# Two-block decoder on one Trainium2 core: a new step sequence for the recurrence pairs, crossed 64-row halves in the triangular inverse, and two-pass suffix sums in the stick-breaking heads

## The reference, cut to what matters

```python
# stick-breaking: 8 heads of 128, twice
u = jnp.where(mask, jax.nn.softplus(z), 0.0)
a = jnp.where(mask, jnp.exp(z - _rev_cumsum(u)), 0.0)   # suffix sums over the keys

# recurrence, per head and token
sa = jnp.einsum('bhvk,bhk->bhv', S, -kk_t)
S = S * w_t[:, :, None, :] + sa[..., None] * (kk_t * a_t)[:, :, None, :] + v_t[..., None] * k_t[:, :, None, :]
o = jnp.einsum('bhvk,bhk->bhv', S, r_t)
```

## Time and profile before

| | us |
|---|---|
| median of 3 runs | 3991.29 (3989.72 to 3993.7) |
| profiled execution, its own time | 3987.37 |
| span of its trace | 3985.6 |
| TensorE busy | 3749.2 |
| VectorE / ScalarE / GpSimd busy | 1779.6 / 1319.2 / 299.8 |
| mean granted TensorE clock | 0.974 of full |

### The profile page before, as it was taken

One profiled execution on the slowest core, in us unless ns is written; L12 is line 12 of the kernel. 1 busy time (PEld: TensorE's weight loads), 2 busy tenths in 40 slices (PEclk: granted clock), 3 DMA queues, 4 the chain that ended last, 5 costly groups with the idle time before them and its releaser, 6 DMA issues.

```text
span 3985.6 us, 52849 instructions
## 1 busy us (share of the span) xinstructions
PE 3749.2 (94%) x22827; PEld 3045.0 (76%) x22827; DVE 1779.6 (45%) x2457; ACT 1319.2 (33%) x2020; POOL 299.8 (8%) x328
## 2 busy tenths in 40 slices
PE   7999999988899999999999999998989998599999
PEld 6777888766688877888887778886867677478887
DVE  4323434444543445443443244344645656445443
ACT  4343322332332232332334332224332323333222
POOL 1011101000110111110100111011000000000001
PEclk9999999999999999999999999998999999799999
DMA  6212333311232332233231132322121221333332
GB/s 205 69 48 69 95 95 95 96 54 45 76 95 91 94 90 87 94 99 97 93 93 43 53 95 88 107 92 82 55 72 50 82 59 54 102 116 89 102 96 68
DMA packets 333229, 337.39 MB, mean 85 GB/s; under 512 B 11858, under 2 KB 323780, under 8 KB 332485
## 3 DMA queue, kind: packets, MB, share of 16 engines
q1 hardware_dynamic: 332578, 333.89, 27.4%
q10 hardware_dynamic: 418, 0.12, 0.0%
HBM read 319.29 MB, written 14.68 MB: 84 GB/s over the span
## 4 chain that ended last, share of the span: by engine, by line
PE 85%; DVE 7%; ACT 5%; issue 2%; DMA 1%; ACTq 0%; POOL 0%; SPq 0%; POOLq 0%; DVEq 0%
PE P L99 84%; DVE lo L117 2%; ACT hi L113 1%; PE P L102 1%; ACT sA L114 1%; DVE rw_S L117 0%; DVE x L117 0%; DVE LG L117 0%; ACT rw_S L114 0%; DVE rw_kk L117 0%; DVE rw_k L117 0%; DVE ds L125 0%; DVE mp L122 0%; ACT L111 0%; DMA scr<-held_dram 0%
## 5 line engine op out<-in xcount | busy, mean ns | idle before, releaser
L117 DVE TENSOR_TENSOR lo<-raw,hi 128x1024 fp32r<-128x1024 f32 (+2 forms) x617 | 739.4, 1199 | 1200.7 <-ACT hi L113 1200.0
L99 PE MATMUL P<-aH,lo 128*128 128x512 f32 x2840 | 1140.5, 402 | 15.0 <-DVE aL L125 7.1
L99 PE MATMUL P<-aL,hi 128*128 128x512 f32 x2840 | 1113.4, 392 | 0.0
L99 PE MATMUL P<-aH,hi 128*128 128x512 f32 x2840 | 1113.3, 392 | 0.0
L113 ACT ACTIVATE hi<-raw 128x1024 fp32r<-128x1024 f32 (+2 forms) x617 | 610.7, 991 | 1055.0 <-PE P L99 1048.3
L99 PEld LDWEIGHTS P<-aH,lo 128*128 128x128 f32 x2840 | 538.5, 190 | 144.8 <-issue 21.0
L99 PEld LDWEIGHTS P<-aL,hi 128*128 128x128 f32 x2840 | 538.5, 190 | 113.1 <-issue 6.4
L99 PEld LDWEIGHTS P<-aH,hi 128*128 128x128 f32 x2840 | 537.4, 189 | 114.0
L99 PE MATMUL P<-bH,lo 128*128 128x512 f32 x1088 | 426.5, 392 | 14.9 <-DVE bL L117 14.9
L99 PE MATMUL P<-bL,hi 128*128 128x512 f32 x1088 | 425.3, 391 | 0.0
L99 PE MATMUL P<-bH,hi 128*128 128x512 f32 x1088 | 425.1, 391 | 0.0
(11 more groups left out here) (276 smaller groups left out, 3906.5 us busy)
## 6 DMA issues: line engine op xcount, KB each, us to landing
raw<-in_w_ffn_in_dram SPq DMA_DIRECT2D x176, 512.0 KB, 3.5
raw<-in_w_in_dram SPq DMA_DIRECT2D x163, 512.0 KB, 3.8
raw<-in_w_ffn_out_dram SPq DMA_DIRECT2D x96, 384.0 KB, 3.0
raw<-in_w_ffn_dram SPq DMA_DIRECT2D x36, 512.0 KB, 3.7
raw<-in_w_o_dram SPq DMA_DIRECT2D x26, 512.0 KB, 3.4
raw<-in_w_ffn_dram SPq DMA_DIRECT2D x32, 384.0 KB, 3.1
raw<-in_w_mem_kv_dram SPq DMA_DIRECT2D x16, 512.0 KB, 3.9
raw<-in_w_ffn_out_dram SPq DMA_DIRECT2D x16, 512.0 KB, 3.4
```

Source lines behind the costliest of these rows:

```text
L99: return self.e.matmul(out, l, r, start=start, stop=stop, skip_group_check=skip) if self.e else Nothing()
L117: return self.e.tensor_tensor(out, a, b, op) if self.e else Nothing()
```

## The change

1. **Sequence of a pair.** The numbers in `pair_steps` change, `rw_square` moves behind projection v and leaves its first half (VectorE product, ScalarE square) as a new step `rw_unit`; `rw_turn_v` moves behind projection r. Banks are dealt out anew.
2. **Crossed halves.** `across` takes the place of `blocks` in `rw_level_a`, `rw_level_b`, `rw_init` and the last part of `rw_solve` (11 of the 16 sets that `blocks` issued in a pair): head h=1 is kept with its two chunks exchanged, so that each of the four combinations of input half and output half occurs, and the results go to two banks, by input half. `rw_level_c` keeps equal halves. A set of 8 products (`Z0`) and a ScalarE copy turn the start value of one head; on VectorE `rw_first` has one operation of 512 columns for two of 256, and two smaller ones.
3. **Stick-breaking sums.** The masked softplus is split into `sH` (ScalarE copy to float32r) and `sL` (VectorE subtraction, written in place over `sA`), in a new step `stick_split`, by banks. The ten float32 products become twenty float32r ones with the constants copied once to `cR`. The first diagonals are zeroed bank by bank.

```diff
-        out += [Step("stick_scores", l, h, u, pe=2.2, lat=8.5, needs=[("qkv", l, h // 2)]),
-                Step("stick_sums", l, h, u, pe=4.4, lat=4.0),
+        out += [Step("stick_scores", l, h, u, pe=2.2, lat=7.0, needs=[("qkv", l, h // 2)]),
+                Step("stick_split", l, h, u, lat=3.5), Step("stick_sums", l, h, u, pe=2.5, lat=4.0),
...
     out = [Step("rw_begin", p, u)]
-    out += proj("k", 1, 0, 1.0)
-    out += [Step("rw_lora", p, u, pe=3.4, lat=4.0), Step("rw_square", p, u, pe=0.9, lat=0.5)]
-    out += proj("v", 2, 1, 3.0)
-    out += [Step("rw_key", p, u), Step("rw_turn_v", p, u, pe=0.45, lat=0.5)]
-    out += proj("r", 0, 2, 4.0)
-    out += [Step("rw_decay", p, u, pe=0.9, lat=3.0)]
-    out += [Step("rw_turn", p, u, n, pe=0.45, lat=(3.0, 0.8, 0.6)[n]) for n in range(3)]
-    out += [Step("rw_gram", p, u, n, pe=1.8, lat=1.2) for n in range(2)]
+    out += proj("k", 1, 1, 0.0)
+    out += [Step("rw_lora", p, u, pe=2.6), Step("rw_unit", p, u)]
+    out += proj("v", 2, 2, 0.0)
+    out += [Step("rw_square", p, u, pe=0.9), Step("rw_key", p, u)]
+    out += proj("r", 0, 1, 0.0)
+    out += [Step("rw_turn_v", p, u, pe=0.45, lat=3.0), Step("rw_decay", p, u, pe=0.9, lat=2.4)]
+    out += [Step("rw_turn", p, u, n, pe=(0.6, 0.45, 0.45)[n], lat=(1.0, 1.0, 0.6)[n]) for n in range(3)]
+    out += [Step("rw_gram", p, u, n, pe=0.9, lat=(1.1, 2.3)[n]) for n in range(2)]
...
     for n in range(1, 6):
-        out += [Step("rw_level_a", p, u, n, pe=0.9, lat=1.8)]
+        out += [Step("rw_level_a", p, u, n, pe=0.5 if n > 1 else 1.2, lat=0.9)]
         if n < 5:
-            out += [Step("rw_level_b", p, u, n, pe=0.9, lat=0.0)]
+            out += [Step("rw_level_b", p, u, n, pe=0.5)]
...
     for ck in range(8):
-        out += [Step("rw_step_a", p, u, ck, pe=0.4, lat=1.0), Step("rw_step_b", p, u, ck, pe=0.7, lat=0.7 if ck < 7 else 1.6)]
+        out += [Step("rw_step_a", p, u, ck, pe=0.25, lat=0.55), Step("rw_step_b", p, u, ck, pe=0.6, lat=0.3 if ck < 7 else 3.0)]
...
+            for n, A in enumerate((m["sH"][u], m["sL"][u])):
+                e.wait_ge(*(S.act_attn, S.dve_attn)[n].at(("stick", l, h, b)))
+                t = e.mm(P[:, B + b, o:o + w], tri, A[:, DIAG[j]:DIAG[j] + w], False, True, True)
...
+    def across(u, l, r, back):
+
+        for q in range(4):
+            for h in range(2):
                 for x in range(2):
-                    rows, cs = slice(64 * x, 64 * x + 64), slice(256 * h + 64 * q, 256 * h + 64 * q + 64)
-                    t = e.mm(P[rows, 3 * u + b, cs], l(h, q)[rows], r(h, q)[rows], True, True, True)
-        return t
+                    s, t = (h ^ x, x) if back else (x, h ^ x)
+                    i = e.mm(P[64 * t:64 * t + 64, 3 * u + s, 64 * q:64 * q + 64], l(h, q, s), r(h, q, s), True, True, True)
+        return i
...
+    def stick_split(l, h, u):
+        A, H = m["sA"][u], m["sH"][u]
+        for b, o, w in FLAT:
+            e.wait_ge(*S.diagonal.at((l, h, b)))
+            e.act(H[:, o:o + w], A[:, o:o + w], ACT.Copy).then_inc(*S.act_attn.up(("stick", l, h, b)))
...
+    def stick_split(l, h, u):
+        A, H, L = m["sA"][u], m["sH"][u], m["sL"][u]
+        for b, o, w in FLAT:
+            e.wait_ge(*S.act_attn.at(("stick", l, h, b)))
+            e.tt(L[:, o:o + w], A[:, o:o + w], H[:, o:o + w].bitcast(F32), ALU.subtract).then_inc(*S.dve_attn.up(("stick", l, h, b)))
```

More of the change, by code:

```diff
@@ L821, in rw_turn @@
     def rw_turn(p, u, n):
-        A, j = m["rw"][u], (0, 2, 1)[n]
+        A = m["rw"][u]
         e.wait_ge(*S.rw_dve[u].at((p, ("KR0", "nb", "kd")[n])))
-        take(3 * u + j)
-        turn(3 * u + j, (A["KR"][:, 0, :], A["aa"], A["S2"])[n], (p, "turn", n), u)
-        rw_free(u, j, S.rw_act[u], (p, "nat", n))
+        if n:
+            j = (2, 0)[n - 1]
+            take(3 * u + j)
+            turn(3 * u + j, (A["aa"], A["S2"])[n - 1], (p, "turn", n), u)
+            rw_free(u, j, S.rw_act[u], (p, "nat", n))
+            return
+        take(3 * u, 3 * u + 1)
+        for q in range(4):
+            for h in range(2):
+                for x in range(2):
+                    t = e.mm(P[half(h, x), 3 * u + h, 64 * q:64 * q + 64],
+                             A["KR"][half(h, 0), 0, 128 * q + 64 * x:128 * q + 64 * x + 64], ident[half(h, 0), half(h, 0)],
+                             True, True, True)
+        t.then_inc(*S.rw_product[u].up((p, "turn", 0)))
+        for j in range(2):
+            rw_free(u, j, S.rw_act[u], (p, "nat", 0))
     def rw_gram(p, u, n):
-        A, js = m["rw"][u], ((0, 2), (1, 0))[n]
+        A, js = m["rw"][u], ((2, 1), (0, 2))[n]
         src = (A["aa"], A["S2"])[n]
@@ L870, in rw_level_a @@
         e.wait_ge(*S.rw_dve[u].at((p, "T", n - 1)))
-        take(3 * u)
-        blocks(u, 0, cut((A["cs"], A["S1"])[n % 2]), cut(A["k"])).then_inc(*S.rw_product[u].up((p, "U", n)))
+        take(3 * u, 3 * u + 1)
+        across(u, plain((A["cs"], A["S1"])[n % 2]), paired(A["k"]), False).then_inc(*S.rw_product[u].up((p, "U", n)))
         rw_free(u, 0, S.rw_act[u], (p, "U", n))
+        rw_free(u, 1, S.rw_act[u], (p, "U", n))
+        if n == 1:
+            take(3 * u + 2)
+            for q in range(4):
+                for x in range(2):
+                    t = e.mm(P[half(1, x), 3 * u + 2, 64 * q:64 * q + 64], paired(A["k"])(1, q, x), ident[half(0, x), half(0, x)],
+                             True, True, True)
+            t.then_inc(*S.rw_product[u].up((p, "Z0")))
+            rw_free(u, 2, S.rw_act[u], (p, "Z0"))
     def rw_level_b(p, u, n):
@@ L878, in rw_level_b @@
         e.wait_ge(*S.rw_dve[u].at((p, "Z", n - 1)))
-        take(3 * u + 1)
-        blocks(u, 1, cut(A["kk"]), cut(A["S0"])).then_inc(*S.rw_product[u].up((p, "dT", n)))
+        e.wait_ge(*S.rw_act[u].at((p, "Z0")))
+        take(3 * u, 3 * u + 1)
+        across(u, plain(A["kk"]), paired(A["S0"]), True).then_inc(*S.rw_product[u].up((p, "dT", n)))
+        rw_free(u, 0, S.rw_dve[u], (p, "T", n))
         rw_free(u, 1, S.rw_dve[u], (p, "T", n))
@@ L1290, in rw_lora, with rw_unit @@
         e.act(A["g"], bank(3 * u), ACT.Copy).then_inc(*mine.up((p, "g")))
[L1292 removed]
+    def rw_unit(p, u):
         A = m["rw"][u]
@@ L1318, in rw_turn, with two @@
         e.wait_ge(*S.rw_product[u].at((p, "turn", n)))
-        e.act(m["rw"][u]["nat"][:, n, :], bank(3 * u + (0, 2, 1)[n]), ACT.Copy).then_inc(*S.rw_act[u].up((p, "nat", n)))
+        out = m["rw"][u]["nat"][:, n, :]
+        if n:
+            e.act(out, bank(3 * u + (2, 0)[n - 1]), ACT.Copy).then_inc(*S.rw_act[u].up((p, "nat", n)))
+        else:
+            e.act(two(out), P[:, 3 * u:3 * u + 2, 0:256], ACT.Copy).then_inc(*S.rw_act[u].up((p, "nat", n)))
+    def two(x):
+        return x.rearrange("p (b f) -> p b f", b=2)
     def rw_level_a(p, u, n):
@@ L1335, in rw_solve @@
         e.wait_ge(*S.rw_product[u].at((p, "Ut")))
-        e.act(A["cs"], bank(3 * u), ACT.Copy).then_inc(*mine.up((p, "Ut")))
+        e.act(two(A["cs"]), P[:, 3 * u:3 * u + 2, 0:256], ACT.Copy).then_inc(*mine.up((p, "Ut")))
         e.wait_ge(*S.rw_dve[u].at((p, "S", 0)))
@@ L1732, in half, with two, eye, level_mask @@
         return x.rearrange("p (h q f) -> p h q f", h=2, f=64)[:, h]
-    def eye():
-        return c[:, K_EYE:K_EYE + 64].unsqueeze(1).to_broadcast([128, 8, 64])
-    def level_mask(u, out, n):
+    def two(x):
+        return x.rearrange("p (b f) -> p b f", b=2)
+    def eye(n):
+        return c[:, K_EYE:K_EYE + 64].unsqueeze(1).to_broadcast([128, n, 64])
+    def level_mask(u, out, n, heads=2):
         mask = c[:, K_LEV + 64 * n:K_LEV + 64 * n + 64].unsqueeze(1).to_broadcast([128, 4, 64])
-        for h in range(2):
+        for h in range(heads):
             t = e.tt(half(out, h), m["rw"][u]["LG"][:, 0, h, :, 0:64], mask, ALU.mult)
@@ L1767, in rw_level_b @@
         e.wait_ge(*S.rw_product[u].at((p, "dT", n)))
-        e.tt(T, T, bank(3 * u + 1), ALU.add).then_inc(*S.rw_dve[u].up((p, "T", n)))
+        e.tt(two(T), two(T), P[:, 3 * u:3 * u + 2, 0:256], ALU.add).then_inc(*S.rw_dve[u].up((p, "T", n)))
     def rw_level_c(p, u, n):
@@ L1927, in stick_scores @@
         A = m["sA"][u]
-        e.wait_ge(*S.dve_attn.at(("softplus", l, h)))
-        for k in DIAG:
-            t = e.above(A[:, k:k + 128])
-        t.then_inc(*S.diagonal.up((l, h, 0)))
+        for b, ks in enumerate(((0,), (512, 896), (1024,))):
+            e.wait_ge(*S.dve_attn.at(("softplus", l, h, b)))
+            for k in ks:
+                t = e.above(A[:, k:k + 128])
+            t.then_inc(*S.diagonal.up((l, h, b)))
     def stick_sums(l, h, u):
```

130 lines of the change are left out of this document (75 added, 55 removed).

## The result

The changed kernel takes 3952.31 us (median of 4 runs, 3949.79 to 3953.18), the kernel before 3992.49 us (4 runs). The ratio is 0.9893 with a 95% interval of 0.9873 to 0.9913: 40 us faster, where 110 were forecast and 3840 to 3930 was the range.

What follows compares the result with a forecast made beforehand. TensorE's time, 94% busy, and its waits were taken to count one to one. Gains 33 + 9 + 33 + 12 + 0 - 4 + 27 = 110 us from 3987.4 gave 3877, forecast as 3881 us; range 3840 to 3930.

Steps and rivals of the forecast that it cites:

- the 15: Sign of being wrong: TensorE waiting more than 15 us in a round of the recurrence stage.
- Tail: Behind the last pair, 84 steps (57 us) of fill cover 31 of 33.8 us of waits; 33 us gained, bounds 20 and 38.
- rw_decay: Sums of `rw_decay`: first wait falls to about 1.2 us, second grows; 24 us against 24.1, nothing gained.
- The second sum: Second `rw_decay` sum of a round: without the fill between the sums its wait grows from 2.0 to 4.8 us.
- The clock rival: Waits at `rw_decay` and the levels keep TensorE at 1.2 GHz for a round's rest, 300 us more: 4180; chance 0.03.
- Levels: Inverse's levels and other small waits: less fill brings VectorE close, 25 us against 21; loss 4, bounds +6 and -25.
- the first rival: VectorE takes what packing gives: waits at levels and chunks cost 39 us, giving 3920 us; chance 0.20.
- Stick-breaking: 16 heads: sums fall from 4.44 to 2.40 us, 33 us, less 5 us at heads 1 and 2; net 27.
- the saving by crossed sets: Recurrence pairs: 11 sets save 0.42 us each; less `Z0`, net 4.2 us a pair, 33 us for eight.
- the returns to fill: Stretches of fill between a pair's own products fall from 139 to 111; 9 us gained, 3 to 11 possible.
- `rw_square`: Its operand is made while projection v runs, so the 12.2 us wait goes; gain 12 us, bounds 9 and 12.
- `Z0`: Added set turning one head's start value: 16 records at 0.029 us, 0.46 us a pair.

Runs made afterwards that it cites:

- experiment 2: Changed kernel with DMAs behind the last pair issued as before or earlier, ScalarE's operations waiting for them placed later in the fill; 3921.94 us, ratio 0.9810.
- Experiment 9: Changed kernel with, on VectorE alone, weight-tile subtractions between projection r and the first decay sum moved behind both sums' work; 3939.02 us, ratio 0.9858.
- experiment 5: Changed kernel with the same 16 products of each crossed set issued by input half, eight then eight, instead of in turns; 3955.45 us, ratio 0.9904.
- Experiment 1: Kernel before with only the stick-breaking part (new split step, its numbers, two-pass sums), recurrence untouched; 3993.4 us, ratio 0.9991.

## Why the prediction was wrong

The direction was right and the size wrong: 40 us for 110. Four terms failed, nearly all of it in waits; a round has 18 us of them (72.4 in four), over the 15 that the prediction named as a sign of being wrong.

*Tail, "31 of the 33.8 us".* The step that failed is "four weight buffers keep TensorE fed while ScalarE waits for the DMA of `vg`". I counted the weights and not the way out: two banks of fill, whose evictions stand on VectorE behind `bL`, which stands behind ScalarE's `bH`, which stands behind the DMA. 57 us of fill gained 10 us, or 7 when the steps are counted in the trace. Shown by experiment 2, where the waits went with ScalarE's place in the order alone.

*rw_decay, "about 1.2 us is left" at the first sum.* I took the wait of 4.35 us before and subtracted the fill put in front of it, as if the operand would stay where it was. It moved: from the start of the first eviction of r to the operand's first operation it took 5.7 us before and 8.1 us after, and the eviction itself began later against the products of r, as the key's work stands ahead of it. The wait is 5.3 to 5.4 us instead of 1.2, four times. Experiment 9 shows that two weight subtractions were 3.8 us of it. The second sum, forecast at 4.8 us, waits 4.84. I had also priced no clock: the sums behind these two waits took 4.6 us more. The clock rival's mechanism exists then, at about 5 us at the sums and not at 300; the granted clock of the second round is 0.95 and was 0.98, that of the four rounds 0.95 and was 0.96.

*Levels, "loss 4 us".* It was 13, inside its bounds, but not by its mechanism. The step that failed is "with less fill, VectorE comes close": the small waits for VectorE and ScalarE went from 18.1 to 17.3 us, and the first rival's 39 us don't show. What came is 14.3 us of `issue`, for which neither the term nor a rival had a place: the trace ties them to blocks of 256 records, and experiment 5 takes 13 us of them away by slowing the sets. That the number lay inside the bounds is luck.

*Stick-breaking, "27 us".* Two parts failed. A pass of 128 columns was taken from the line through wider ones; with 20 passes the sums take 2.87 us in the mean and not 2.40, 7.5 us in all, inside the bounds that I gave it. At the full clock it is 2.73 us (two heads from 336.85 to 342.32): passes of 128 columns took 0.06 or 0.11 us, and some of 256 columns 0.17 for 0.12. And "beside fill, except at heads 1 and 2" is wrong: TensorE also waits for the evictions of `q` (2.1 and 3.6 us a layer, none before) and once more for the memory attention's `mp` (2.9 and 2.0 us, of which 1.0 is given back at the next), and heads 1 to 3 have no fill. Experiment 1 has the same waits, so they come with this part of the change; whether with its split or with its order was not separated. Of the 23 us of shorter products 15 went into waits by the gaps of the two stages; some 5 more went into slower products around them and the borders of the stages, which I have not separated.

What held: the saving by crossed sets (0.98 to 0.56 us a set in the mean of 88, 33 us net, where 0.92 to 0.51 was forecast), the returns to fill, `rw_square`, `Z0`, the second decay sum. All are durations of TensorE's own work or a wait whose cover was a full projection. What failed was in three terms a cover whose other queues I hadn't followed, and in the levels a stop that I hadn't thought of.

## What to carry to other kernels

Fill covers a wait only if everything that the fill itself needs on the other engines can run during the wait: its weight copies, and its evictions, of which only as many can be outstanding as there are banks. Before counting it as cover, write down for each in-order queue what stands ahead of the fill's next instruction, and split an operation that waits for a DMA from the issue of that DMA. And fill is worth most where the wait is a computation of fixed length (the decay sums: 80 steps there took away 31 us of waits) and least where it is already blocked.

After making products shorter, look at TensorE's waits marked `issue`. If they stand a fixed number of records apart, here 256, the supply of instructions may be at its limit, and then further packing only lengthens them, as here: 15 us of packing were worth 1.

## What the runs showed of the hardware

In the changed kernel the starts of crossed products come in bursts (timeline of TensorE, at a border of two sets):

```profile
2973.01 0.22 PE L99 MATMUL P<-rw_S,rw_kk 64*64 64x64 f32 x1
2973.01 0.22 PE L99 MATMUL P<-c,rw_k 64*64 64x64 f32 x1
2973.01 0.22 PE L99 MATMUL P<-rw_S,rw_kk 64*64 64x64 f32 x1
2973.06 0.22 PE L99 MATMUL P<-c,rw_k 64*64 64x64 f32 x1
2973.07 0.23 PE L99 MATMUL P<-rw_S,rw_kk 64*64 64x64 f32 x1
2973.07 0.22 PE L99 MATMUL P<-c,rw_k 64*64 64x64 f32 x1
```

Every 0.058 us there are up to four starts, one for each combination of input and output half, and in the equal-half sets of `rw_level_c` two in the same time (0.93 us for 32 records, as in the earlier trace rows). The starts of one burst are about 7 ns apart. The four combinations run side by side, and products of the next set begin while the last of one are under way. The Trainium skill's page "TensorE: Matmul & The Clock Gate", section "Wait — 56ns, not 53.3ns?", says that starts never come closer than about 25 ns; for products of 64 rows and 64 columns this trace shows several within 0.01 us.

The stops of experiment 5 give an estimate of how fast TensorE is fed: in the changed kernel the shortest distance between two of them is 3.65 us (3140.59 to 3144.24) for 256 records, 14 ns each. A crossed set has 32 product records and as many weight loads in 0.51 us, 8 ns each, so a run of crossed sets alone is faster than that.

The clock after one and the same wait can differ. Behind the 2.93 us wait at the first spatial product (`sb,c`) the granted clock was 0.72 over the next 12 us in the changed kernel. In experiment 9, with the same wait of 2.93 us at the same products, it was low for more than 20 us (the first two windows below), and from `wsn` to the end it took 8 us longer. In experiment 2 the wait was 2.13 us and the clock stayed at 1.00:

```profile
3428.00:3440.00 12.00, 11.41 (x30) 7.27 (x31) 4.78 (x7) 2.95 (x4) 0.00 (x0) 0.54 0.37 114
3440.00:3452.00 12.00, 12.00 (x31) 7.21 (x30) 2.14 (x4) 5.20 (x7) 0.00 (x0) 0.50 0.21 66
```

```profile
3424.00:3437.00 13.00, 12.12 (x54) 7.49 (x55) 5.88 (x8) 5.28 (x7) 0.00 (x0) 1.00 0.46 158
```

Each is one profile, and why the two differ wasn't tested. It limits what differences of under 10 us between these kernels can be given to an edit.
